# Weight chunks in two transfers, last products in other banks, and the block sums of the gated product on GpSimd: one core, hybrid decoder layer

## What is computed

```python
def _swiglu(h, w_gu, w_down):
    a, b = jnp.split(h @ w_gu, 2, axis=-1)      # w_gu: 1024 x 5632
    return (jax.nn.silu(a) * b) @ w_down        # w_down: 2816 x 1024

x = x + 0.5 * _swiglu(_rmsnorm(x, ffn1_norm[l]), ffn1_w_gu[l], ffn1_w_down[l])
... attention block ...
x = x + 0.5 * _swiglu(_rmsnorm(x, ffn2_norm[l]), ffn2_w_gu[l], ffn2_w_down[l])
```

## Time and profile before

| | us |
|---|---|
| median of 3 runs (lowest, highest) | 2198.47 (2197.08, 2198.56) |
| profiled execution, its own time | 2196.08 |
| its span in the trace | 2194.2 |
| PE busy | 2160.8 (98% of the span) |
| DVE busy | 1578.4 (72%) |
| ACT busy | 908.6 (41%) |
| POOL busy | 453.1 (21%) |

### The profile page before, as it was taken

One profiled execution on the slowest core, in us unless ns is written; L12 is line 12 of the kernel. 1 busy time (PEld: TensorE's weight loads), 2 busy tenths in 40 slices (PEclk: granted clock), 3 DMA queues, 4 the chain that ended last, 5 costly groups with the idle time before them and its releaser, 6 DMA issues.

```text
span 2194.2 us, 26286 instructions
## 1 busy us (share of the span) xinstructions
PE 2160.8 (98%) x9968; PEld 1733.5 (79%) x9968; DVE 1578.4 (72%) x1809; ACT 908.6 (41%) x1433; POOL 453.1 (21%) x396
## 2 busy tenths in 40 slices
PE   8999999999999999999999999999999999999998
PEld 7787888888887777777778888888887888888887
DVE  7878888888888688877535343354877888888885
ACT  6333333333335677846442111233233333344332
POOL 3013322223323122221000000012013322233320
PEclk9999999999999999999999999999999999999999
DMA  5111111111112300011112111131111111111113
GB/s 172 62 50 57 58 58 58 49 35 52 58 58 84 115 20 29 20 48 39 39 21 77 48 58 48 48 125 39 49 49 57 58 58 58 43 37 57 58 58 96
DMA packets 46733, 126.54 MB, mean 58 GB/s; under 512 B 3405, under 2 KB 20077, under 8 KB 46352
## 3 DMA queue, kind: packets, MB, share of 16 engines
q1 hardware_dynamic: 44704, 112.60, 15.5%
q10 hardware_dynamic: 912, 10.11, 1.2%
q0 software_dynamic: 992, 2.15, 0.5%
HBM read 116.42 MB, written 9.87 MB: 58 GB/s over the span
## 4 chain that ended last, share of the span: by engine, by line
PE 78%; DVE 9%; DMA 5%; POOL 4%; issue 3%; ACT 1%; POOLq 0%; DVEq 0%; SPq 0%; ACTq 0%
PE ps L2129 76%; DMA raw<-in_weights 4%; POOL raw L789 2%; POOL q_sum L786 2%; DVE h_lo L1387 1%; DVE q_lo L1557 1%; DVE xT L1523 1%; DVE q_lo L1546 1%; DVE b_sum_lo L1510 1%; DVE a_full L1590 1%; POOL q_sum L792 1%; DVE tok_lo L1439 1%; PE ps L2744 0%; DVE xT L1731 0%; PE ps L2679 0%
## 5 line engine op out<-in xcount | busy, mean ns | idle before, releaser
L2129 PE MATMUL ps<-tok_hi,q_hi 128*128 128x512 f32 x1008 | 392.5, 389 | 0.0
L2129 PE MATMUL ps<-tok_lo,q_hi 128*128 128x512 f32 x1008 | 392.1, 389 | 0.0
L2129 PE MATMUL ps<-tok_hi,q_lo 128*128 128x512 f32 x1008 | 392.1, 389 | 0.0
L2129 PE MATMUL ps<-h_hi,w_hi 128*128 128x512 f32 x960 | 373.1, 399 | 1.7 <-ACT h_hi L1112 1.1
L2129 PE MATMUL ps<-h_lo,w_hi 128*128 128x512 f32 x960 | 363.9, 391 | 0.7 <-DVE h_lo L2041 0.6
L1523 DVE TENSOR_TENSOR xT<-xT,ps 128x1024 f32<-128x1024 f32 x252 | 302.1, 1216 | 33.8 <-PE ps L2129 23.1
L2129 PE MATMUL ps<-h_hi,w_lo 128*128 128x512 f32 x960 | 305.5, 391 | 0.0
L2129 PEld LDWEIGHTS ps<-tok_hi,q_hi 128*128 128x128 f32 x1008 | 189.2, 188 | 40.2 <-issue 1.1
L2129 PEld LDWEIGHTS ps<-h_hi,w_hi 128*128 128x128 f32 x960 | 179.9, 188 | 51.3 <-issue 15.7
L2129 PEld LDWEIGHTS ps<-tok_hi,q_lo 128*128 128x128 f32 x1008 | 189.2, 188 | 39.4
L2129 PEld LDWEIGHTS ps<-tok_lo,q_hi 128*128 128x128 f32 x1008 | 189.2, 188 | 39.1
(11 more groups left out here) (309 smaller groups left out, 3682.0 us busy)
## 6 DMA issues: line engine op xcount, KB each, us to landing
raw<-in_weights SPq DMA_DIRECT2D x56, 1024.0 KB, 5.0
raw<-in_weights SPq DMA_DIRECT2D x83, 512.0 KB, 3.5
x_keep<-xT ACTq DMA_DIRECT2D x1, 4096.0 KB, 12.4
x_back<-x_keep ACTq DMA_DIRECT2D x1, 4096.0 KB, 12.1
x_nat<-in_x SPq DMA_DIRECT2D x7, 512.0 KB, 7.4
out<-y_nat SPq DMA_DIRECT2D x7, 512.0 KB, 3.2
toe_keep<-toe_row ACTq DMA_DIRECT2D x2, 704.0 KB, 5.8
m_nat<-in_mem SPq DMA_DIRECT2D x1, 1024.0 KB, 8.0
```

Of the source, the lines that this page charges most:

```text
L2129: return pe.matmul(o, a, b, start=start, stop=stop, skip_group_check=True)
```

## The change

Every chunk is loaded by two DMAs of 512 KB, one per half. A tile's chunk is laid out anew (`seven`), so that its first half holds the blocks a11 and a21 and the second half a12 and a22. Each half is loaded when the part that last reads its predecessor in the buffer is split: behind part 4 and part 6 of a tile, part 3 and part 6 of a pair (`half_end`). Readers wait for the halves that they read.

The four sums of activation blocks move from DVE to POOL. For pair g from 2 on, t1, b12 and t2 are made behind the weight sums of part 5 of pair g - 1, that is during the preceding odd tile; t4 is made behind S1 and S2 of the next even tile's part 1. For pair 1 all four stand behind the weight sum S3 of tile 4 part 4.

The last group's output tiles use PSUM pairs in the order 1, 0, 2, 3, repeated, in the first feed-forward; in the second, m = 0 and 1 use pairs 1 and 0 and the rest 2 and 3. The turns of the output are put further behind: none after m = 0 and 1, then 0, 1, 2, then 3 and 4 together after m = 5, then 5 and 6.

```diff
+def end_pair(f, m):
+    return (1, 0, 2, 3)[m % 4] if f == 0 or m < 2 else 2 + m % 2
+def half_end(c, half):
+    kind, of = CHUNK[c]
+    return part_at(kind, of, {"tile": (4, 6), "pair": (3, 6), "down": (1, 3)}[kind][half]) + 1
...
             def chunks(f):
                 for c in range(CHUNKS):
-                    if c == 0:
-                        sp.wait_ge(split_done, U_HALVES[f] + 6)
-                    elif c == 1:
-                        sp.wait_ge(unit_done, U_HALVES[f] + 6)
-                    else:
-                        sp.wait_ge(part_split, NPART * f + chunk_end(c - 2))
-                    sp.dma_start(raw2[c % 2][:], weights[chunk_at(f, c):chunk_at(f, c) + 2].rearrange("a p n -> p a n")
-                                 ).then_inc(raw_in[c % 2], 16)
+                    for half in range(2):
+                        if c == 0:
+                            sp.wait_ge(split_done, U_HALVES[f] + 6)
+                        elif c == 1:
+                            sp.wait_ge(unit_done, U_HALVES[f] + 6)
+                        else:
+                            sp.wait_ge(part_split, NPART * f + half_end(c - 2, half))
+                        sp.dma_start(raw2[c % 2][:, half, :], weights[chunk_at(f, c) + half]
+                                     ).then_inc((raw_in, chunk_in)[c % 2][half], 16)
...
-                    after_chunk(pool, f, c)
+                    after_chunk(pool, f, c, *((0, 1) if kind == "tile" else (0,) if p < 4 else (1,)))
...
+            def pair_sums(f, g, last):
+                begin = 4 * (ND * f + g - 1)
+                b12, t1, t2, t4 = a_full[2 * g % 4][:, T1], b_full(g, 3), b_full(g, 5), b_full(g, 6)
+                if g == 1:
+                    pool.wait_ge(up_scaled, PLAIN * (f + 1))
+                elif not last:
+                    pool.wait_ge(part_done, NPART * f + part_at("pair", g - 1, 4) + 1)
+                    pool.wait_ge(glu_done, (TILE_COUNT - 2) * f + a_count(2 * g + 1) - 3)
+                else:
+                    pool.wait_ge(part_done, NPART * f + part_at("pair", g - 1, SEVEN - 1) + 1)
+                    pool.wait_ge(glu_done, (TILE_COUNT - 2) * f + a_count(2 * g + 1) - 2)
+                if not last:
+                    nc.gpsimd.tensor_tensor(t1, b12, b_full(g, 0), ALU.subtract).then_inc(a_summed, 1)
+                    pool.wait_ge(a_summed, begin + 1)
+                    nc.gpsimd.tensor_tensor(b12, b_full(g, 1), b12, ALU.subtract).then_inc(a_summed, 1)
+                    nc.gpsimd.tensor_tensor(t2, b_full(g, 1), t1, ALU.subtract).then_inc(a_summed, 1)
+                else:
+                    pool.wait_ge(a_summed, begin + 3)
+                    nc.gpsimd.tensor_tensor(t4, b_full(g, 2), t2, ALU.subtract).then_inc(a_summed, 1)
+
             def weights_sums(f):
                 for n in range(NPART):
                     for i, name in enumerate(sums_for(n)):
                         weights_sum(f, n, i, name)
+                    kind, of, p, c = PARTS[n]
+                    if kind == "tile" and of == PLAIN and p == 4:
+                        pair_sums(f, 1, False)
+                        pair_sums(f, 1, True)
+                    if kind == "pair" and of < ND and p == 5:
+                        pair_sums(f, of + 1, False)
+                    if kind == "tile" and of > PLAIN and of % 2 == 0 and p == 1:
+                        pair_sums(f, (of - 2) // 2, True)
...
+                if kind == "tile":
+                    after_chunk(act, f, c, 0 if p < 5 else 1)
+                elif kind == "pair":
+                    after_chunk(act, f, c, *((0,) if p < 3 else (0, 1) if p == 3 else (1,)))
...
-                    if kind == "tile" and of % 2 == 0 and p in (1, 2):
-                        pair_sums(f, (of - 2) // 2, p == 2)
...
                 if p == 0:
                     pe.wait_ge(a_ready, A_COUNT * (f + 1) - 2)
-                    for m in range(2):
-                        pe.wait_ge(down_added, G + m - 1)
-                        whole(m, 0)
+                    pe.wait_ge(seven_added, 3 * TILES7 * (f + 1))
+                    whole(0, 0)
+                    pe.wait_ge(glu_done, (TILE_COUNT - 2) * (f + 1))
+                    whole(1, 0)
                 pe.wait_ge(a_ready, A_COUNT * (f + 1))
                 for m in (2 * p, 2 * p + 1):
                     if p:
-                        pe.wait_ge(down_added, G + m - 1)
+                        pe.wait_ge(down_added, G + m - (1 if f or p == 1 else 3))
...
-            ffn(1, lambda m: y_turn(m - 1) if m else None)
+            def y_behind(m):
+                for k in ((), (), (0,), (1,), (2,), (3, 4), (5,), (6,))[m]:
+                    y_turn(k)
+            ffn(1, y_behind)
```

More of the change, by code:

```diff
@@ L498, in layer @@
         raw_in = [sem(f"raw_in{i}") for i in range(NRAW)]
+        chunk_in = [sem(f"chunk_in{i}") for i in range(2)]
         hi_done, split_done, unit_done = sem("hi_done"), sem("split_done"), sem("unit_done")
@@ L581, in after_slot, with after_chunk @@
                 eng.wait_ge(unit_done, U_HALVES[f] + (4, 4, 5, 6)[n])
-        def after_chunk(eng, f, c):
-            eng.wait_ge(raw_in[c % 2], 16 * ((U_HALVES[f] + 6) // 2 + CHUNKS // 2 * f + c // 2 + 1))
+        def after_chunk(eng, f, c, *halves):
+            for half in halves:
+                if c % 2:
+                    eng.wait_ge(chunk_in[half], 16 * (CHUNKS // 2 * f + c // 2 + 1))
+                else:
+                    eng.wait_ge(raw_in[half], 16 * ((U_HALVES[f] + 6) // 2 + CHUNKS // 2 * f + c // 2 + 1))
         def o_tile(i):
@@ L774, in weights_sum @@
                 if kind == "tile":
-                    a11, a12, a21, a22 = (raw2[c % 2][:, r, cols] for r in range(2) for cols in BOTH)
+                    a11, a21, a12, a22 = (raw2[c % 2][:, r, cols] for r in range(2) for cols in BOTH)
                     to = slot[:]
@@ L1486, in whole_lo @@
                 nc.vector.tensor_tensor(a_lo[t % 4][:], a_full[t % 4][:], a_hi[t % 4][:].bitcast(F32), ALU.subtract).then_inc(a_ready, 1)
-            def pair_sums(f, g, late):
-                if g == 1:
-                    dve.wait_ge(up_scaled, PLAIN * (f + 1))
-                else:
-                    dve.wait_ge(glu_done, (TILE_COUNT - 2) * f + a_count(2 * g + 1) - 2)
-                    dve.wait_ge(part_done, NPART * f + part_at("pair", g - 1, SEVEN - 1) + 1)
-                begin = 4 * (ND * f + g - 1)
-                b12, t1, t2, t4 = a_full[2 * g % 4][:, T1], b_full(g, 3), b_full(g, 5), b_full(g, 6)
-                if not late:
-                    nc.vector.tensor_tensor(t1, b12, b_full(g, 0), ALU.subtract).then_inc(a_summed, 1)
-                    dve.wait_ge(a_summed, begin + 1)
-                    nc.vector.tensor_tensor(b12, b_full(g, 1), b12, ALU.subtract).then_inc(a_summed, 1)
-                else:
-                    nc.vector.tensor_tensor(t2, b_full(g, 1), t1, ALU.subtract).then_inc(a_summed, 1)
-                    dve.wait_ge(a_summed, begin + 3)
-                    nc.vector.tensor_tensor(t4, b_full(g, 2), t2, ALU.subtract).then_inc(a_summed, 1)
             def pair_lo(f, g, i):
@@ L2241, in seventh, with down_mm @@
                 last.then_inc(part_done, 1)
-            def down_mm(m, q, hi, lo, t, first, final, halves=BOTH, within=None):
+            def down_mm(pair, hi, lo, t, first, final, halves=BOTH, within=None):
                 for cols in halves:
@@ L2247, in down_mm @@
                         within()
-                    mm(ps[:, 2 + m % 2, cols], hi, a_hi[t % 4][:, cols], first, False)
-                    mm(ps[:, 2 + m % 2, cols], hi, a_lo[t % 4][:, cols], False, False)
+                    mm(ps[:, pair, cols], hi, a_hi[t % 4][:, cols], first, False)
+                    mm(ps[:, pair, cols], hi, a_lo[t % 4][:, cols], False, False)
                 for cols in halves:
-                    last = mm(ps[:, 2 + m % 2, cols], lo, a_hi[t % 4][:, cols], False, final)
+                    last = mm(ps[:, pair, cols], lo, a_hi[t % 4][:, cols], False, final)
                 return last
@@ L2304, in whole @@
                     at_ = P * (2 * q + m % 2)
[L2305 removed]
+                    return down_mm(end_pair(f, m), q_hi[n % NQ][:, at_:at_ + P], q_lo[n % NQ][:, at_:at_ + P], 2 * g + q, q == 0, q == 1,
                                    halves, within)
@@ L2892, in down, with seven @@
         return [w_down[f * P:(f + 1) * P] for f in range(GT * g, GT * g + GT)]
+    def seven(t):
+        gate, up = tile(t)
+        return [np.concatenate([w[:, half * 512:half * 512 + 512] for w in (gate, up)], axis=1) for half in range(2)]
     def pair(g):
@@ L2899, in swiglu_units @@
     plain = tile(0) + tile(1) + tile(2)[:1] + down(0) + tile(2)[1:] + tile(3)
-    chunks = [unit for kind, of in CHUNK for unit in (tile(of) if kind == "tile" else pair(of))]
+    chunks = [unit for kind, of in CHUNK for unit in (seven(of) if kind == "tile" else pair(of))]
     return plain, chunks
```

26 lines of the change are left out of this document (14 added, 12 removed).

## The result

The changed kernel takes 2171.42 us (median of 4 runs, 2171.34 to 2171.68) against 2197.77 for the kernel before beside it (2195.73 to 2198.56): a ratio of 0.9882, 95% interval 0.9865 to 0.9899. The change makes the kernel 1.2% faster. The forecast was 2174.9. The span of the profiled execution fell from 2194.2 to 2169.5 us, by 24.7; the forecast's sum was 23.6. (The medians differ by 26.3: the profiled execution of the kernel before was 1.7 us faster than its median, that of the changed kernel lay on it.)

A forecast was written before the change was run, and what follows sets the result against it. PE, busy 98% of the span, was taken as the bound, with only its waits to win. Terms 13.8 + 2.5 + 3.0 + 4.3 = 23.6 us off 2198.5 gave 2174.9 us; range 2166 to 2185.

The forecast's parts named there:

- pair 1: First pair of each feed-forward: large gap and half clock replaced by smaller waits, 1.25 us gained twice, 2.5 us.
- the first end: Last group of the first feed-forward: no gap, DVE starts earlier, then PE waits about 2 us for DVE; 3.0 us gained.
- Part 1, the transfers: Steady periods: data come 6.9 us earlier, PE's waits at pair parts 0 and 1 go; 13.8 us gained.
- Part 2, the sums: Four sums per pair, DVE to POOL: the engines take turns; 2.5 us gained at pair 1, cost 0 later.
- Cost 0, because that lead hides it: Pairs from 2 on: `q_lo`, 3 us ahead of PE, hides POOL's sums; without the lead up to 1.3 us a period.
- Part 3, the banks: Last groups of both feed-forwards: the new bank order avoids PE's gap, gaining 3.0 us in the first, 4.3 in the second.
- rival B: New waits at pair 1's parts 5 and 7 and the first end: three clock falls of 1.7 us, 2180.0; chance 0.2.
- The second end: Last group of the second feed-forward: gap of 2.77 us and half clock of 1.7 go, less 0.2; 4.3 us gained.
- A: DVE and POOL don't hold each other where it counts: pair 1 gains 4.5 us twice, 2168.4; chance 0.15.
- C: Steady periods: POOL's sums keep the addition of pair part 0 late, 6.4 us less gain, 2181.3; chance 0.1.
- D: Odd tile's part 5 to next even tile's part 3: sums use up DVE's lead, 2.4 us a period, about 2229; chance 0.05.
- E: No change: PE meets an equal wait at pair part 0, pair 1 and the ends offset each other, 2198; chance 0.03.

The follow-up runs named there:

- e9: Kernel before with each chunk loaded as two halves issued at the old moment, readers waiting only for halves they need; sums and banks as before: 2171.74 us.
- e10: e9 with every reader of a chunk waiting for both halves: 2193.33 us.
- e5: Changed kernel with both half transfers, from the third chunk on, waiting for the last part of the chunk two before: 2173.47 us.
- e2: Kernel before with the early transfers by halves alone, sums on VectorE and old order of the banks: 2169.78 us.
- e1: Changed kernel with all four sums of each pair back on VectorE at their old places: 2166.61 us.
- e4: Changed kernel with only pair 1's four sums back on VectorE, the other pairs' sums staying on POOL: 2167.73 us.
- e6: Changed kernel with two more sums on POOL ahead of the first one of each pair from pair 2 on: 2171.05 us.
- e3: Changed kernel with the order of the banks, its waits and the order of the transposes undone: 2172.82 us.
- e11: e8 with acc_lo on VectorE instead of POOL and TensorE's norm products ahead of the rest of the next unit: 2165.28 us.
- e8: e1 and e7 together, with VectorE's low part of the unit after next moved into the norm's chain: 2167.55 us.
- e7: Changed kernel with 12 of the next unit's products put ahead of the last h_lo wait in the first unit behind the first feed-forward: 2171.47 us.

## Why the prediction was right, and where it was not

**The total** (2174.9 against 2171.4) and the direction were right, and of the four terms the largest was near: 14.9 for 13.8. The others measured 3.6 for 2.5 (pair 1), 1.5 for 3.0 (the first end) and 4.4 for 4.3 (the second). So the sum of 23.6 came within 1.1 of the measured 24.7, with errors that cancel in part: two terms were 1.1 too small each and one 1.5 too large. That it is so close is partly luck. The other 2.4 us of the difference are the start of the sum: the forecast took the median to lie 2.4 us above the profiled execution, and in the changed kernel it does not. Two terms were put on the wrong part of the change: the gain at pair 1 on the sums, and most of the gain at the ends on the banks. Both are the transfers' work, and since all three parts were made together, this does not show in the total.

**Part 1, the transfers.** "So data come 6.9 us earlier ... Both waits go" is true of the trace, but most of the 6.9 was not needed. The 1.5 us of the first half, which lands sooner and has a semaphore of its own, are enough for the whole gain of the periods (e9: losses 0, e10: 5.0). The 5.4 of the earlier issue only add lead there: `q_lo` of pair 2 part 0 is ready 0.88 us ahead of PE in e5 and 1.85 in the changed kernel. Whether the earlier issue would be enough without the faster landing was not run. It pays in pair 1: 2.0 us by e5's losses (3.6 for 2.6, twice) and by the times of e9 and e2.

**Part 2, the sums.** The forecast set pair 1's 1.25 us of gain to the sums. The gain there is the transfers' (loss 4.5 to 1.1, e2), and the sums give 1.5 of it back (1.1 to 2.6). The alternation was foreseen: the token splits, sums and low parts of the rows above come in the order worked out, `q_lo` of part 5 at 162.50 where I had put 163.25, and PE waited there. The sizes, in issue time, were off: 1.39 at part 5 for 2.0, 0.31 at part 7 for 1.3. Between them I missed 0.72 us at part 6. The profile names no engine for that wait; PE goes on 0.1 us after the addition `a_up_half` ends (165.37 + 0.67), which is queued behind the late `q_lo`, and 0.66 us of loss is in this place with the sums on DVE too. Net the gain was 1.8 us each. "Cost 0, because that lead hides it" for the pairs from 2 on holds (e1 and e4, e6). e3 against e2 shows what the sums cost in time, 3.0 us. That is on the side of the rule cited from the Trainium skill (page SBUF — State Buffer, "Who interferes with whom"), and the rows above (150.74 to 162.50) agree with it.

**Part 3, the banks.** "3.0 us" for the first end measured 1.5. The mechanism was right, PE waited 2.12 us for DVE's `h_lo` where I had put 2; the missing 1.5 is the clock, which fell behind it (in e1, where it did not fall, the same end gives 2.9). That is rival B at one of its three places. The second end, 4.3, measured 4.4, but e2 gives 3.0 of that with the transfers alone, about half of it the clock's, and 1.4 of the 1.5 at the first end. The forecast computed the ends against the kernel before and did not ask what Part 1 leaves of them.

**Rivals.** A (no holding), C and D (more holding) did not occur; E neither. Of B's three falls of the clock one came, behind the first end. The range held the time.

## What to carry to other kernels

Split a transfer where its first reader needs only a part, and give each part its own semaphore: with two halves issued together nothing differed but which half the readers wait for, and that was worth 21.6 us (e10 against e9). Before counting a move of work to an idle engine as relief, ask whether the engine relieved had been waited for: here DVE's lateness was late data, and the move cost 3 us. And when a gap on the critical engine is filled and the time stays, follow the wait to where it was handed on: after two steps it pointed at the start of a chain (`acc_lo` and the products that read it), and an earlier start of the chain won 2.3 us (e11 against e8). Filling alone had won nothing (e7), or cost 0.9 (e8 against e1).

## What the runs showed of the hardware that was not expected

The clock's fall is not settled by the length of the gap ahead of it. Gaps of 2.5 to 2.7 us were followed by it in seven of nine cases (before three of four, e10 three of four, e7 its one at 711.93), those of 2.1 us behind the first feed-forward in four profiled executions of six (both of the changed kernel, e4, e6; not e1, e5). The gap of 2.24 us at 722.45 in e8 was not, nor was any of 1.2 to 1.4 us within the feed-forwards. What decides at 2.1 us stays open. It is not the kernel alone, as the mean granted clock of every run shows. In e4 it is 1.000 in the run of 2166.91 us and 0.999 in those of 2167.68 to 2168.00; in e5 1.000 at 2171.68 and 2172.95 and 0.999 at 2173.99 and 2174.03; in e7 1.000 at 2170.12 and 0.999 at 2171.42 to 2171.89. The fall cost 1.5 to 1.7 us each time in the profiled executions.

And the holding goes both ways: POOL's 512-column sum takes 1.29 us alone and took 3.35 beside a token split (151.92 and 150.74). The split's own row is 3.38, where one that was held less took 2.28; its start had stood for POOL's `q_sum` until 151.96. So each row contains its wait for the other engine.
